# Two transformer blocks on one core: both directions of a recurrence level in one product, head norms and rotations in rounds

## The chip, the cores and the metric

The program runs on one core of a Trainium2 chip, in one launch. The metric is the time of one execution in microseconds (us) as the device measures it. TensorE (PE) multiplies, VectorE (DVE) and ScalarE (ACT) work on the elements, GpSimd (POOL) makes a part of the low halves and starts some loads, and SyncE (SP) starts the weight loads.

## The reference

The input has 256 tokens of width 1024, and a context has another 256. A first block (feed-forward, attention, feed-forward) comes first, then two layers of a second block. The change touches the second block only. Cut to what matters there:

```python
def gla_chunked(q, k, v, logf, s0):        # both directions; heads of 128, chunks
    g = cumsum(logf)
    o = (q * exp(g)) @ state + tril((q*decay) @ k.T) @ v
def hgrn_readout(o, g_raw, norm_g):
    return rms_norm(o, norm_g) * silu(g_raw)

for l in range(2):                         # second_block
    ...                                    # h = adaln_norm(x), hc = adaln_norm(context)
    q = apply_axial_rope(rms_norm(heads(q_raw), q_norm_g[l]), rope)   # heads of 64
    k = apply_axial_rope(rms_norm(heads(k_raw), k_norm_g[l]), rope)
    o_a = window_attention(q, k, v, kc, vc, sink)
    o_h, _, _ = hgrn_bidir(hgrn_q(qh_raw), kf, lff, kb, lfb, vh, s_f, s_b)
    o_hr = hgrn_readout(o_h, gh_raw, hgrn_norm_g[l])
    o_f = fourier_mix(four_raw)
    y = (sigmoid(gate_raw) * [o_f, o_a, o_hr] @ w_branch[l]).sum() @ w_out[l]
    x = x + gate2 * y
    x = x + gate5 * square(relu(adaln_norm(x) @ w_ff1[l])) @ w_ff2[l]
```

In layer 0 the context goes through the same steps as the tokens (512 columns in all); in layer 1 only its keys, values and final states are needed, so that most products there have 256 columns.

## The kernel before

**Weights.** Each fp32 weight block of 128x1024 is loaded into `wr` by SP (four buffers), ACT copies it to `wh` (high half, line 419) and DVE or POOL subtracts to get `wl` (low half, line 435; three buffers of each). A product is then three matmuls, lines 452, 455 and 457: high x high, high x low, low x high. ACT and the subtracting engine run two blocks ahead of PE. Which engine makes a low half depends on a place in the stream: `self.W.step(("pool on", l))` gives all blocks behind it to POOL.

**Order.** PE, ACT and DVE each have a program of their own, written out by hand and joined by semaphores. Every engine executes in its own order. `Ring` hands out buffers in turn: `main` and `aux` are four PSUM banks each, `tm` has three SBUF buffers, `rm` has one. Layer l does, in this order:
1. forget gates, queries and values of the recurrence;
2. the **recurrence levels** (`pe_recurrence`, `act_recurrence`, `dve_recurrence`). Level lv joins blocks of 2^lv tokens, for directions z = 0 and 1. For each z, PE multiplies K[z] by one half of the columns of Q[z] (line 1579, eight 128x64 products per sequence; layer 0 has two sequences, tokens and context). DVE scales Q[z] and K[z] by the forget factors (`dve_raise`, lines 1636 and 1639), writes the products into `AT` under a mask (`dve_pairs_out`, line 1664) and joins the factors (`dve_join`, line 1652). Level 7 (line 1572) and the states and outputs (`pe_outputs`) follow;
3. `pe_gate_h`, then the **head stage**: four readouts (norm of the recurrence's output, times a gate), values, five heads (K at j = -1, Q at 0 to 3: tile, norm, rotation), four tiles for the Fourier branch, and the Fourier products;
4. the **units** of the attention (`pe_units`: 16 with a row of scores each, in layer 0 eight more for the context), then the branches, the output and the feed-forward.

**Filling.** The 24 gate tiles of a layer depend on nothing in stages 2 to 4, and so fill holes: `Fill` deals them out in halves of 12 matmuls. `inside(n)` gives up to n halves in the recurrence until `last` (24 halves in layer 0, 32 in layer 1), `all` gives two. `OUT_FILLS` are the halves within `pe_outputs`. In the levels each z is followed by one half, in layer 1 for z = 1 by two.

**Head stage.** `pipeline(gens, 3, fill.all)` keeps three generators alive and calls each in turn, each call followed by up to two halves. A norm is: square by ACT (`act_scale`), a column sum by PE (line 1761), scale and offset by DVE out of PSUM (line 1789), Ln and Exp by ACT (lines 1778, 1780), one Newton step by DVE (lines 1792, 1794, 1796) and the product with gain and root (line 1800). A head is first copied out of PSUM (line 1880). Its rotation is one PE product (line 1863) and three DVE operations (lines 1888, 1892, 1894). `pe_head` after its norm reads:

```python
yield
...
w.wait_ge(*self.c("s_v").at((key, 4)))
ins = e.matmul(self.aux.item((key, "turn"))[:, 0:256], self.const["perm"], dst[:, 0:256], ...)
```

so that PE waits for the end of that head's DVE chain. `fill.all` has used up the gate halves by the second head of either layer.

## Time and profile before

| | us |
|---|---|
| median of 3 runs | 2222.09 |
| lowest, highest | 2217.89, 2223.20 |
| profiled execution | 2222.47 |
| its span, first to last instruction | 2220.7 |
| PE busy in the span | 2063.4 (93%) |
| DVE / ACT / POOL busy | 1275.5 / 926.2 / 597.6 |
| mean granted TensorE clock | 0.966 |

The span is 1.8 us shorter than the execution's own time, which is 0.4 us over the median. "Busy" of PE counts matmuls from start to modelled end, also when they run at the lower clock (1.2 instead of 2.4 GHz), so a stretch can be 100% busy and still slow. The page's second part shows where the clock was below 1. The rows on which the prediction rests follow behind the change.

### The profile page before, as it was taken

The page shows a single profiled execution, that of the slowest core. Times are in us where ns is not written, and L with a number is a line of the kernel's source. Part 1 is how long each engine was busy: PE and PEld are TensorE (multiplying, and loading weights), DVE is VectorE, ACT ScalarE, POOL GpSimd, SP SyncE. Part 2 cuts the span into 40 slices and gives each one's busy share as a digit, 9 for nine tenths or more (in the row PEclk, how much of TensorE's full clock was granted, in tenths as well). Part 3 has the DMA queues.
Part 4 walks back from the last instruction along what each step waited for, and adds up shares of the span by engine and source line. Part 5 has one row for each costly group of instructions (what it writes and reads, how often), then busy time and mean ns, then how long its engine had stood idle before and what let it go on. Part 6 is the DMA issues. An engine that isn't in the chain of part 4 may idle for free.

```text
span 2220.7 us, 31129 instructions
## 1 busy us (share of the span) xinstructions
PE 2063.4 (93%) x12564; PEld 1803.7 (81%) x12564; DVE 1275.5 (57%) x1973; ACT 926.2 (42%) x1497; POOL 597.6 (27%) x341
## 2 busy tenths in 40 slices
PE   7799788899989999989899899999999996888999
PEld 7799676799978998867578788888778986578999
DVE  5578896578855860343774583353367735575410
ACT  5344335455445123431553442243263342455643
POOL 0211000000000001432024355455400043046887
PEclk9899999899989999999899999999999999899999
DMA  7887371366722111211013244465422332024554
GB/s 260 248 274 259 128 243 44 119 236 218 257 86 95 48 48 67 93 69 48 1 57 114 95 152 142 152 206 192 161 90 91 114 115 85 20 92 143 185 190 153
DMA packets 84640, 299.21 MB, mean 135 GB/s; under 512 B 9993, under 2 KB 13201, under 8 KB 84113
## 3 DMA queue, kind: packets, MB, share of 16 engines
q1 hardware_dynamic: 64512, 231.76, 30.4%
q0 software_dynamic: 17280, 60.88, 8.6%
q10 hardware_dynamic: 2704, 4.57, 0.6%
q8 instruction: 100, 1.64, 0.3%
q14 instruction: 44, 0.35, 0.1%
HBM read 296.11 MB, written 4.11 MB: 135 GB/s over the span
## 4 chain that ended last, share of the span: by engine, by line
PE 81%; DVE 9%; ACT 4%; issue 2%; DMA 2%; POOL 2%; ACTq 0%; DVEq 0%; POOLq 0%
PE ps L457 21%; PE ps L452 21%; PE ps L455 21%; PE ps L1579 3%; PE ps L1056 2%; PE ps L1016 1%; PE ps L1033 1%; DVE wl L435 1%; PE ps L959 1%; PE ps L964 1%; PE ps L961 1%; PE ps L536 1%; DMA naskew<-narel 1%; POOL wl L435 1%; ACT wh L419 1%
## 5 line engine op out<-in xcount | busy, mean ns | idle before, releaser
L452 PE MATMUL ps<-HH,wh 128*128 128x256 f32 (+1 forms) x2336 | 769.9, 330 | 25.3 <-ACT HH L1284 10.7
L457 PE MATMUL ps<-HH,wl 128*128 128x256 f32 (+1 forms) x2336 | 757.2, 324 | 26.4 <-DVE wl L435 23.1
L435 POOL TENSOR_TENSOR wl<-wr,wh 128x1024 fp32r<-128x1024 f32 x214 | 519.8, 2438 | 918.1 <-ACT wh L419 903.6
L455 PE MATMUL ps<-HL,wh 128*128 128x256 f32 (+1 forms) x2336 | 756.7, 324 | 1.4 <-DVE HL L1300 1.4
L419 ACT ACTIVATE wh<-wr 128x1024 fp32r<-128x1024 f32 x440 | 460.1, 1052 | 338.1 <-PE ps L457 300.2
L452 PEld LDWEIGHTS ps<-HH,wh 128*128 128x128 f32 x2336 | 453.9, 194 | 66.0 <-issue 25.7
L457 PEld LDWEIGHTS ps<-HH,wl 128*128 128x128 f32 x2336 | 453.4, 194 | 61.6 <-DVE wl L435 25.0
L455 PEld LDWEIGHTS ps<-HL,wh 128*128 128x128 f32 x2336 | 453.6, 194 | 38.3 <-DVE HL L1300 3.4
L435 DVE TENSOR_TENSOR wl<-wr,wh 128x1024 fp32r<-128x1024 f32 x226 | 274.3, 1223 | 148.7 <-ACT wh L419 146.7
L457 PE MATMUL ps<-HIDH,wl 128*128 128x512 f32 (+1 forms) x512 | 173.1, 338 | 0.0
L452 PE MATMUL ps<-HIDH,wh 128*128 128x512 f32 (+1 forms) x512 | 172.8, 338 | 0.0
L455 PE MATMUL ps<-HIDL,wh 128*128 128x512 f32 (+1 forms) x512 | 172.3, 336 | 0.0
L2119 DVE SCALAR_TENSOR_TENSOR X<-ps,MOD,X 128x256 f32<-128x256 f32 x64 | 28.8, 480 | 246.8 <-PE ps L457 246.8
L805 POOL DMA_DIRECT2D WM<-wmod x68 | 37.7, 554 | 412.4 <-DVE MOD L832 372.9
L832 DVE CUSTOM_DVE_ANT_0 PROD<-WM,COND 128x1024 f32<-128x1024 f32 x104 | 130.3, 1261 | 1.3
L455 PEld LDWEIGHTS ps<-HIDL,wh 128*128 128x128 f32 x512 | 96.1, 188 | 11.8
L452 PEld LDWEIGHTS ps<-HIDH,wh 128*128 128x128 f32 x512 | 96.1, 188 | 11.7
L457 PEld LDWEIGHTS ps<-HIDH,wl 128*128 128x128 f32 x512 | 96.0, 188 | 11.7
L457 PE MATMUL ps<-NHH,wl 128*128 128x256 f32 x352 | 98.7, 280 | 0.2 <-DVE wl L435 0.2
L452 PE MATMUL ps<-NHH,wh 128*128 128x256 f32 x352 | 98.4, 280 | 0.0
L455 PE MATMUL ps<-NHL,wh 128*128 128x256 f32 x352 | 98.1, 279 | 0.0
L2186 DVE TENSOR_TENSOR HIDL<-tm,HIDH 128x512 fp32r<-128x512 f32 (+1 forms) x64 | 75.3, 1176 | 37.9 <-ACT HIDH L2170 37.9
(250 smaller groups left out, 2759.1 us busy)
## 6 DMA issues: line engine op xcount, KB each, us to landing
wr<-wstream SPq DMA_DIRECT2D x440, 512.0 KB, 3.3
WM<-wmod POOLq DMA_DIRECT2D x68, 512.0 KB, 3.9
X<-wmod POOLq DMA_DIRECT2D x28, 512.0 KB, 5.4
NAB<-naskew POOLq DMA_DIRECT2D x16, 128.0 KB, 7.1
dilskew<-lines POOLq DMA_DIRECT2D x1, 2048.0 KB, 22.5
DILB<-dilskew POOLq DMA_DIRECT2D x2, 1024.0 KB, 12.6
COND<-cond ACTq DMA_DIRECT2D x2, 1024.0 KB, 4.8
CT<-consts POOLq DMA_DIRECT2D x1, 1152.0 KB, 9.6
```

Source lines behind the costliest of these rows:

```text
L419: ins = e.activation(self.WH[i % NSPL][:, :], self.WR[n % NRAW][:, :], ACT.Copy)
L435: ins = e.tensor_tensor(self.WL[i % NSPL][:, :], self.WR[n % NRAW][:, :], self.WH[i % NSPL][:, :].bitcast(F32), ALU.subtract)
L452: e.matmul(out, wh, xh, start=i == 0, stop=False)
L455: e.matmul(out, wh, xl, start=False, stop=False)
L457: ins = e.matmul(out, wl, xh, start=False, stop=i == n_k - 1)
L536: ins = e.matmul(self.aux.item((key, "sum"))[:, 0:T], self.ones, self.tm.item((key, "sq", i))[:, 0:T], start=i == 0, stop=i == n - 1)
L805: e.dma_start(self.mod_buffer(z, i), src).then_inc(self.mod_sem[i], 16)
L832: ins = e.tensor_tensor_reduce(out=P, in0=self.mod_buffer(z, i), in1=S, scale=1.0, scalar=0.0, op0=ALU.mult, op1=ALU.add, accum_out=self.M ...
L1056: ins = e.matmul(b[off:off + 64, 128 * u.a:128 * u.a + 128], self.V2[:, c, off:off + 64], p[:, 128 * c:128 * c + 128], start=c == 0, stop= ...
L1579: ins = e.matmul(b[:, c:c + 64], K[:, h, at:at + 128], self.side(Q[:, h, at:at + 128], 1 << lv, 1 - z), start=True, stop=True)
L2119: ins = e.scalar_tensor_tensor(out=self.X[:, d, sl], in0=self.main.item(k)[:, sl], scalar=self.MOD[:, l, mod_i + d, c:c + 1], in1=self.X[: ...
L2186: ins = e.tensor_tensor(hl[:, f - nf * part, :], v, hh[:, f - nf * part, :].bitcast(F32), ALU.subtract)
```

## The change

**Levels 0 to 6, one product for both directions.** A new mixed K lies in `R`: for each block of the level, the K of direction 0 or 1 (`act_mixed_k`, two ACT copies per level, which wait for the level before). `Q[0]` and `Q[1]` now lie side by side as `QQ`, and `mixed_q` reads them alternately by blocks. Per sequence and half, PE does four 128x128 products (line 1567 of the new file) in place of two times four 128x64. DVE raises both K first, then both Q; the masked copies are whole (4x128 columns, `r_cp` per s and a).

**Fewer halves inside.** `last` goes from (24, 32) to (16, 24) halves; the levels get `REC_FILLS`, `OUT_FILLS` depends on the layer. `fill.some` gives two halves per round in layer 0 and one in layer 1, up to 44, and the units get what is left.

**Rounds.** `pipeline` starts one generator per round, calls each live one once per round, the new one before the last, and fills once per round. The Fourier tiles move into the readouts, the order is Q0, Q1, K, values, Q2, Q3. The norm uses a mean matrix (`mean128`, `mean64`); Ln reads PSUM with eps as bias; the four DVE operations (lines 1823 to 1830 of the new file) read PSUM where needed, and the copy (line 1880) and the scaling (line 1789) are gone. Mean, root, DVE chain and rotation of a head fall in successive rounds.

**Low halves.** `("pool on", l)` moves from before the head stage to behind the units: DVE makes those 48 low halves (POOL has 167 in place of 215, DVE 274 in place of 226).

```diff
-OUT_FILLS = (2, 2, 2)
+REC_FILLS, OUT_FILLS = ((2, 1, 2, 1, 2, 1, 2), (2, 3, 2, 3, 2, 3, 2)), ((1, 1, 1), (2, 2, 1))
...
-        for lv in range(8):
-            for z in range(2):
-                K, Q = self.K[z], self.Q[z]
-                w.wait_ge(*self.c("r_up").at((l, lv, z)))
-                for s in self.seqs(l):
...
-                        for a in range(2):
-                            at = 256 * s + 128 * a
-                            for h in range(4):
-                                c = 64 * (4 * a + h)
-                                ins = e.matmul(b[:, c:c + 64], K[:, h, at:at + 128],
-                                               self.side(Q[:, h, at:at + 128], 1 << lv, 1 - z), start=True, stop=True)
...
-                fill(1 + z * l)
+        for lv in range(7):
+            w.wait_ge(*self.c("r_km").at((l, lv)))
+            w.wait_ge(*self.c("r_up").at((l, lv, 1)))
+            for s in self.seqs(l):
+                for a in range(2):
...
+                    for h in range(4):
+                        ins = e.matmul(self.aux.item(key)[:, 128 * h:128 * h + 128], self.R[:, h, at:at + 128],
+                                       self.mixed_q(h, at, 1 << lv), start=True, stop=True)
+                    ins.then_inc(*self.c("r_mm").mark((l, lv, s, a)))
+            fill(REC_FILLS[l][lv])
...
+    def mixed_q(self, h, at, hh):
+
+        ap = self.QQ[:, 0, h, at:at + 128]
+        return bass.AP(ap.tensor, ap.offset, [list(ap.ap[0]), [2 * hh, 64 // hh], [2048 + hh, 2], [1, hh]])
...
+    def act_mixed_k(self, e, w, l, lv):
+
+        T = 256 if l else 512
+        w.wait_ge(*self.c("r_mm").at((l, lv - 1, self.seqs(l)[-1] if lv else 0, 1)))
+        for z in range(2):
+            for x in ([self.c("r_ku").at((l, lv, z))] if lv else self.forget_done(l)):
+                w.wait_ge(*x)
+            ins = e.activation(self.head_side(self.R[:, :, 0:T], 1 << lv, z), self.head_side(self.K[z][:, :, 0:T], 1 << lv, z),
+                               ACT.Copy)
+        ins.then_inc(*self.c("r_km").mark((l, lv)))
...
+        for lv in range(7):
             for z in range(2):
-                self.dve_raise(e, w, l, lv, z)
-                if lv < 7:
-                    for s in self.seqs(l):
-                        self.dve_pairs_out(e, w, l, lv, z, s)
-                    self.dve_join(e, w, l, lv, z)
-                fill(1 + z * l)
...
+                self.dve_raise_k(e, w, l, lv, z)
+            for z in range(2):
+                self.dve_raise_q(e, w, l, lv, z)
+            for s in self.seqs(l):
+                for a in range(2):
+                    self.dve_pairs_out(e, w, l, lv, s, a)
+            for z in range(2):
+                self.dve_join(e, w, l, lv, z)
+            fill(REC_FILLS[l][lv])
...
-        e.activation(r, v, ACT.Ln, scale=-2.0).then_inc(*self.c("s_a").mark((key, 0)))
+        e.activation(r, self.aux.item((key, "mean"))[:, 0:T], ACT.Ln, bias=self.vec("eps", 0)).then_inc(
+            *self.c("s_a").mark((key, 0)))
...
+    def dve_scale(self, e, w, key, T, g, v, src, dst):
...
+        e.scalar_tensor_tensor(out=v, in0=m, scalar=EPS, in1=r, op0=ALU.add, op1=ALU.mult).then_inc(*sv.mark((key, 0)))
...
+        e.scalar_tensor_tensor(out=v, in0=v, scalar=-0.5, in1=r, op0=ALU.mult, op1=ALU.mult).then_inc(*sv.mark((key, 1)))
...
+        e.scalar_tensor_tensor(out=r, in0=v, scalar=1.5, in1=r, op0=ALU.add, op1=ALU.mult).then_inc(*sv.mark((key, 2)))
...
+        e.scalar_tensor_tensor(out=dst, in0=src, scalar=g, in1=r, op0=ALU.mult, op1=ALU.mult).then_inc(*sv.mark((key, 3)))
...
-        self.W.step(("pool on", l))
         self.pe_gate_h(e, w, l, T, rT)
-        pipeline([self.pe_readout(e, w, l, h, T) for h in range(4)], 3, fill.all)
-        pipeline([self.pe_values(e, w, l, keys)] + [self.pe_head(e, w, l, j, T, keys) for j in range(-1, 4)]
-                 + [self.pe_four_in(e, w, l, g, T, rT) for g in range(4)]
-                 + [self.pe_fourier(e, w, l, g, T, self.rings["p2"]) for g in range(4)], 3, fill.all)
+        pipeline([self.pe_readout(e, w, l, h, T, rT) for h in range(4)]
+                 + [self.pe_head(e, w, l, j, T, keys) for j in (0, 1, -1)] + [self.pe_values(e, w, l, keys)]
+                 + [self.pe_head(e, w, l, j, T, keys) for j in (2, 3)]
+                 + [self.pe_fourier(e, w, l, g, T, self.rings["p2"]) for g in range(4)], fill.some)
         self.pe_units(e, w, layer_units(l), self.unit_rings(2), lambda u: self.layer_qk(l, u),
                       [self.c("hd_cp").at(("v2", l))], fill.all)
+        self.W.step(("pool on", l))
...
+    def some(self):
+
+        for _ in range(min(2 if self.last == 16 else 1, 44 - self.n)):
+            self.half()
...
-def pipeline(gens, width, fill):
+def pipeline(gens, fill):
+
 
     gens, active = list(gens), []
     while gens or active:
-        if gens and len(active) < width:
+        turns = list(active)
+        if gens:
             active.append(gens.pop(0))
-        for g in list(active):
+            turns.insert(max(len(turns) - 1, 0), active[-1])
+        for g in turns:
             if next(g, "end") == "end":
                 active.remove(g)
-            fill()
+        fill()
```

PE in the levels of layer 0 before: one direction's products of two sequences, 12 matmuls of a half gate tile, the other direction's products (Q_87 and Q_88 are the two Q, K_85 and K_86 the two K).

```order
L1579 MATMUL ps<-Q_87,K_85 128x64 x16
L452 MATMUL ps<-HH,wh 128x512
L455 MATMUL ps<-HL,wh 128x512
L457 MATMUL ps<-HH,wl 128x512
...
L1579 MATMUL ps<-Q_88,K_86 128x64 x16
```

The same place after, with the waits of the first and the later groups of four:

```order
L1567 MATMUL ps<-QQ,R 128x128 [waits s_r_cp,s_r_up,s_r_km]
L1567 MATMUL ps<-QQ,R 128x128 x3
L1567 MATMUL ps<-QQ,R 128x128 [waits s_r_cp]
...
L452 MATMUL ps<-HH,wh 128x512
L455 MATMUL ps<-HL,wh 128x512
L457 MATMUL ps<-HH,wl 128x512
```

Sixteen 128x128 products stand for 32 of 128x64. The start of a level now waits for DVE's raised Q (`r_up`), for ACT's mixed K (`r_km`) and for the masked copies (`r_cp`), once per level instead of twice.

DVE between two heads of layer 1 before: norm, product with the root, copy of the next head out of PSUM, rotation of the last.

```order
L1789 TENSOR_SCALAR tm<-ps 128x256 [waits s_s_mm]
L1792 TENSOR_TENSOR tm<-tm,rm 128x256 [waits s_s_a]
L1794 TENSOR_TENSOR tm<-tm,rm 128x256 [waits s_s_v]
L1796 SCALAR_TENSOR_TENSOR rm<-tm,rm 128x256 [waits s_s_v]
L1800 SCALAR_TENSOR_TENSOR Q_101<-Q_101,V,rm 128x256 [waits s_s_v]
L1880 COPY Q_101<-ps 128x256 [waits s_dense]
L1888 TENSOR_TENSOR tm<-ps,CT 128x256 [waits s_hd_mm,s_hd_v]
L1892 TENSOR_TENSOR Q_101<-Q_101,CT 128x256 [waits s_s_v]
L1894 TENSOR_TENSOR Q_101<-Q_101,tm 128x256 [waits s_hd_v]
```

DVE in one round of heads of layer 1 after:

```order
L1823 SCALAR_TENSOR_TENSOR Q_100<-ps,rm 128x256 [waits s_s_a]
L1826 SCALAR_TENSOR_TENSOR Q_100<-Q_100,rm 128x256 [waits s_s_v]
L1828 SCALAR_TENSOR_TENSOR rm<-Q_100,rm 128x256 [waits s_s_v]
L1830 SCALAR_TENSOR_TENSOR Q_100<-ps,V,rm 128x256 [waits s_s_v]
L435 TENSOR_TENSOR wl<-wr,wh 128x1024 [waits s_hi,s_dense] x3
L1942 TENSOR_TENSOR tm<-ps,CT 128x256 [waits s_hd_mm]
L1946 TENSOR_TENSOR Q_100<-Q_100,CT 128x256 [waits s_s_v]
L1948 TENSOR_TENSOR Q_100<-Q_100,tm 128x256 [waits s_hd_v]
```

The rotation belongs to the head one round further on; low halves stand where POOL made them before.

PE at the same two places, first before and then after (line 452 opens a tile, line 457 needs the low half):

```order
L1863 MATMUL ps<-Q_101,CT 128x256 [waits s_s_v,s_hd_cp]
L1761 MATMUL ps<-tm,CT 128x256 [waits s_s_sq]
L452 MATMUL ps<-HH,wh 128x256 [waits s_hi]
...
L457 MATMUL ps<-HH,wl 128x256 [waits s_lo_pool]
...
L1863 MATMUL ps<-Q_101,CT 128x256 [waits s_s_v,s_hd_v]
```

```order
L452 MATMUL ps<-HH,wh 128x256 [waits s_hi,s_s_v]
...
L457 MATMUL ps<-HH,wl 128x256 [waits s_lo_dve]
...
L1915 MATMUL ps<-Q_100,CT 128x256
L452 MATMUL ps<-HH,wh 128x512 [waits s_gate]
...
L1796 MATMUL ps<-tm,CT 128x512 [waits s_s_sq]
```

The rotation product (line 1863, now 1915) no longer has a wait of its own here: the tile ahead of it already waited for that DVE chain (`s_s_v`), because it takes the PSUM bank that the chain gives back.

## Rows read from the trace of the kernel before

**Rows 1.** Page, part 4: the chain that ended last, by engine.

```profile
PE 81%; DVE 9%; ACT 4%; issue 2%; DMA 2%; POOL 2%; ACTq 0%; DVEq 0%; POOLq 0%
```

**Rows 2.** Windows by stage: length, busy us of each engine, PEclk, DMA, GB/s.

```profile
730.95:819.40 88.45, 88.45 (x617) 81.64 (x616) 67.36 (x75) 10.80 (x14) 0.00 (x0) 1.00 0.12 42
856.00:1054.10 198.10, 186.66 (x785) 147.82 (x783) 68.31 (x88) 60.79 (x85) 63.36 (x26) 0.98 0.21 72
1054.10:1130.10 76.00, 68.75 (x353) 43.92 (x352) 58.53 (x155) 46.19 (x136) 0.00 (x0) 0.89 0.00 1
1700.39:1755.50 55.11, 55.11 (x479) 55.11 (x478) 53.76 (x68) 13.62 (x21) 0.00 (x0) 1.00 0.27 96
1755.50:1905.60 150.10, 125.31 (x825) 114.56 (x823) 63.27 (x93) 54.71 (x91) 53.06 (x22) 0.94 0.29 99
1905.60:1957.50 51.90, 45.50 (x225) 27.48 (x224) 36.84 (x103) 31.36 (x88) 0.00 (x0) 0.87 0.00 1
```

**Rows 3.** Timeline, PE, levels: start, us, line, tile, count.

```profile
724.64 3.74 PE L1555 MATMUL ps<-Q,R 128*128 128x128 f32 x32
...
730.95 3.69 PE L1579 MATMUL ps<-Q,K 128*128 128x64 f32 x32
734.44 0.48 PE L452 MATMUL ps<-HH,wh 128*128 128x512 f32 x1
...
737.26 3.69 PE L1579 MATMUL ps<-Q,K 128*128 128x64 f32 x32
...
1702.10 0.36 PE L452 MATMUL ps<-HH,wh 128*128 128x256 f32 x1
...
1703.61 1.89 PE L1579 MATMUL ps<-Q,K 128*128 128x64 f32 x16
```

**Rows 4.** Timeline, DVE, levels of layer 0.

```profile
735.82 1.22 DVE L1636 TENSOR_TENSOR K<-K,F 128x1024 f32<-128x1024 f32 x1
736.95 2.47 DVE L1664 COPY_PREDICATED AT<-LM,ps 128x512 f32<-128x512 uint8 x2
...
746.69 1.20 DVE L435 TENSOR_TENSOR wl<-wr,wh 128x1024 fp32r<-128x1024 f32 x1
...
762.49 1.31 DVE L1664 COPY_PREDICATED AT<-LM,ps 128x512 f32<-128x512 uint8 x2
```

**Rows 5.** Waits of PE, head stages: total, times, longest; layer 0, then 1.

```profile
PE ps L1863 <- DVE Q L1800: 6.6, 4, 1.8
...
PE ps L1863 <- DVE Q L1800: 9.9, 4, 3.0
PE ps L1863 <- DVE K L1800: 4.4, 1, 4.4
PE ps L1761 <- ACT tm L1771: 3.8, 3, 1.6
...
PE ps L457 <- POOL wl L435: 2.4, 3, 1.0
```

**Rows 6.** Timeline, all engines, one head of layer 1.

```profile
1860.04 0.42 DVE L1888 TENSOR_TENSOR tm<-ps,CT 128x256 f32<-128x256 f32 x1 [0.59 <-PE ps L1863]
...
1863.50 0.43 DVE L1796 SCALAR_TENSOR_TENSOR rm<-tm,rm 128x256 f32<-128x256 f32 x1
1863.64 2.48 POOL L435 TENSOR_TENSOR wl<-wr,wh 128x1024 fp32r<-128x1024 f32 x1 [4.81 <-PE ps L457]
1863.96 2.44 DVE L1800 SCALAR_TENSOR_TENSOR Q<-Q,V,rm 128x256 f32<-128x256 f32 x1
...
1867.85 0.42 DVE L1888 TENSOR_TENSOR tm<-ps,CT 128x256 f32<-128x256 f32 x1 [1.11 <-PE ps L1863]
```

**Rows 7.** Timeline, PE, first units of layer 1.

```profile
1913.06 1.09 PE L1033 MATMUL ps<-CT,s 128*128 128x128 f32 x4 [5.46 <-DVE s L1150]
1914.08 2.07 PE L1016 MATMUL ps<-K,Q 64*128 64x512 f32 x2
...
1929.51 1.12 PE L1016 MATMUL ps<-K,Q 64*128 64x512 f32 x2
```

More of the change, by code:

```diff
@@ new lines, in dve_raise @@
+    def dve_raise(self, e, M, z, hh, u, c0, c1):
+        if c1 - c0 == 512:
+            m, f = (t.rearrange("p h t -> p (h t)") for t in (M[:, :, :], self.F[z][:, :, :]))
+            m, f = self.side(m, hh, u), self.side(f, hh, 1 - u)[:, :, 0]
+            return e.tensor_tensor(m, m, bc(f, 2, hh), ALU.mult)
+        m = self.head_side(M[:, :, c0:c1], hh, u)
+        f = self.head_side(self.F[z][:, :, c0:c1], hh, 1 - u)[:, :, :, 0]
+        return e.tensor_tensor(m, m, bc(f, 3, hh), ALU.mult)
@@ L1750, in act_out, with pe_scale @@
             self.aux.release(key, self.c("r_ca"), (l, "out", s, hp))
-    def pe_scale(self, e, w, key, T, over):
+    def pe_scale(self, e, w, key, T, mean):
         self.tm.take((key, "sq"))
         yield
-        self.aux.take((key, "sum"))
-        for x in self.aux.before((key, "sum")):
+        self.aux.take((key, "mean"))
+        for x in self.aux.before((key, "mean")):
             w.wait_ge(*x)
         w.wait_ge(*self.c("s_sq").at(key))
-        ins = e.matmul(self.aux.item((key, "sum"))[:, 0:T], self.const[over], self.tm.item((key, "sq"))[:, 0:T],
+        ins = e.matmul(self.aux.item((key, "mean"))[:, 0:T], self.const[mean], self.tm.item((key, "sq"))[:, 0:T],
                        start=True, stop=True)
@@ L1765, in pe_scale @@
         self.rm.take(key)
-        self.tm.take((key, "v"))
+        yield
     def act_scale(self, e, w, key, T, src, ready):
@@ L1805, in pe_gate_h @@
+        self.rm.release(key, sv, (key, 3))
     def pe_gate_h(self, e, w, l, T, rhs):
@@ L1820, in act_gate_h, with pe_readout @@
             self.main.release(key, self.c("gh"), (l, h))
-    def pe_readout(self, e, w, l, h, T):
-        yield from self.pe_scale(e, w, ("ro", l, h), T, "ones")
+    def pe_readout(self, e, w, l, h, T, rhs):
+        c = W_IN["four"] + 128 * h
+        self.pe_tile(e, w, l, ("four", l, h), [(c, c + 128)], T, rhs)
+        yield from self.pe_scale(e, w, ("ro", l, h), T, "mean128")
+        self.tm.take(("ro", l, h))
+        yield
+        yield
     def act_readout(self, e, w, l, h, T):
+        self.make_high(e, w, (("four", l, h), 0))
         yield from self.act_scale(e, w, ("ro", l, h), T, self.O[:, h, 0:T], self.o_done(l))
+        yield
         w.wait_ge(*self.c("o_gate").at((l, h)))
@@ L1829, in act_readout @@
         ins.then_inc(*self.c("oh_hi").mark((l, h)))
+        yield
     def dve_readout(self, e, w, l, h, T):
         o, key = self.O[:, h, 0:T], ("ro", l, h)
-        yield from self.dve_scale(e, w, key, T, 128, self.vec("hgrn_norm_g_2", l), o)
-        w.wait_ge(*self.c("s_v").at((key, 4)))
+        self.make_low(e, w, "lo_dve", (("four", l, h), 0))
+        for x in self.o_done(l):
+            w.wait_ge(*x)
+        w.wait_ge(*self.c("dense").at(("four", l, h)))
+        e.tensor_copy(self.FR[:, h, 0:T], self.main.item(("four", l, h))[:, 0:T]).then_inc(*self.c("four").mark((l, h)))
+        self.main.release(("four", l, h), self.c("four"), (l, h))
+        yield
+        yield
+        for x in self.tm.before(key):
+            w.wait_ge(*x)
+        self.dve_scale(e, w, key, T, self.vec("hgrn_norm_g_2", l), self.tm.item(key)[:, 0:T], o, o)
+        self.tm.release(key, self.c("s_v"), (key, 2))
+        w.wait_ge(*self.c("s_v").at((key, 3)))
         w.wait_ge(*self.c("gh").at((l, h)))
         e.tensor_tensor(o, o, self.GH[:, h, 0:T], ALU.mult).then_inc(*self.c("o_gate").mark((l, h)))
+        yield
         w.wait_ge(*self.c("oh_hi").at((l, h)))
```

218 lines of the change are left out of this document (102 added, 116 removed).

## Prediction

> **What bounds the kernel now.** I read the page's chain by engine first [rows 1]: PE carries 81% of it, so what counts is PE's work, PE's idle time, and PE's clock. Then I took one window for each stage the change touches [rows 2]: window length, busy time of each engine, granted clock. They split the case in two.
>
> - Levels: 88.45 us in layer 0, 55.11 in layer 1, PE busy for all of both at clock 1.00. Here only fewer matmuls, or fewer gate halves, can shorten PE; DVE with 67.36 and 53.76 us busy is right behind, in layer 1 only 1.35 us behind.
> - Head stages and units: PE is idle for 198.10 - 186.66 = 11.4 us (heads, layer 0), 76.00 - 68.75 = 7.3 (units), 150.10 - 125.31 = 24.8 (heads, layer 1) and 51.90 - 45.50 = 6.4 (units), 49.9 us in all. The clock was below 1: busy time times (1 - clock) is time lost to it, 3.7, 7.6, 7.5 and 5.9 us, 24.7 in all. Together 74.6 us are the most that better order there can give, unless a matmul disappears.
>
> The waits [rows 5] say what the heads wait for: the rotation product on the last operation of the same head's norm (6.6 us in layer 0; 9.9 + 4.4 in layer 1), the mean on ACT's square (3.8), low halves of POOL (2.4). One head in the timeline [rows 6] shows how such a wait gets long: a whole period is 1867.85 - 1860.04 = 7.8 us, and line 1800, an operation of 0.43 us like its neighbour, takes 2.44 us after it started 0.32 us behind a low half of POOL. At the units [rows 7] PE starts after a gap of 5.46 us and then runs the same two matmuls in 2.07 us that later take 1.12: the clock's lower level after the gap.
>
> **Levels, PE's side.** The products of one direction take 734.44 - 730.95 = 3.49 us in layer 0 for 32 matmuls of 128x64, and 728.13 - 724.64 = 3.49 was the pace of 32 of 128x128 just before [rows 3] (the rows show 3.7 us with the drain). So a product costs the same with twice the columns, about 0.109 us, and halving the number halves the time: seven levels go from 48.9 to 24.4 us. In layer 1 one direction takes 1.7 us (half as many), 23.9 goes to 12.0. A half gate tile takes 737.26 - 734.44 = 2.82 us and 1703.61 - 1702.10 = 1.51 [rows 3]. 3 of 14 leave the levels of layer 0, 4 of 21 those of layer 1; they are moved, not saved: 8.5 and 6.0 us come back later.
>
> **Levels, DVE's side.** PE would need 24.4 + 11 x 2.82 = 55.4 us in layer 0 and 12.0 + 17 x 1.51 = 37.7 in layer 1. DVE needs more, so it is now the bound. Its raises stay (28 per layer; 1.13 us from one start to the next) and its joins; low halves, one per two gate halves at 1.14 us [rows 4], fall by 1.5 and 2. The masked copies stay in number, but the first two levels' took 1.12 us each (2.47 for two) and later ones 0.62 (1.31 for two) [rows 4]; they now write whole tiles, like later ones, if the strided writing was the reason: -0.5 x 8 = -4.2 us, in layer 1 -2.1. From both sides: they save nothing, or these figures. DVE: 67.4 - 1.7 - 4.2 = 61.5 us, and 53.8 - 2.3 - 2.1 = 49.4 us. Levels of layer 0 with two halves are PE's again (3.5 + 5.6 = 9.1 us against 8.8 for DVE), +1.2. So 62.7 and 49.4 us against 88.45 and 55.11. With the moved halves the gain is 25.7 - 8.5 = **17.3 us** in layer 0 and 5.7 - 6.0 = **0** in layer 1. PE then idles 7 and 12 us in them.
>
> ACT's new copies (two per level, of 128x1024 or half) find an engine that is busy 10.80 of 88.45 and 13.62 of 55.11 us [rows 2]. I cost them at nothing: they run while DVE raises Q, which is waited for anyway, and behind them on ACT stand only high halves that are made ahead. Exposed, they would cost the level's start: a second per level, 14 us, as the far bound.
>
> PE's idling has a price where it drops the clock. Level stages show 1.00 without gaps; units show 0.87 and 0.89 with gaps of 5 us. The new gaps are 1 us per level in layer 0 and 1.7 in layer 1, and I allow **-3 us** for them, between nothing and the whole layer-1 stage at half rate (below).
>
> **Head stages.** A round in layer 1 is one tile (24 products of 0.12 us, 2.9 us), one gate half (1.5), a mean and a rotation: about 4.7 to 5.2 us of PE. DVE has four norm operations and three rotation operations of 0.43 us, with 0.46 between starts (3.2), and 1.5 low halves (1.7): 4.8 to 5.4 us. Before, a head took 7.8 us [rows 6], since its steps followed each other within one call and the halves had run out by the second head. Now each wait has a whole round in between: what PE waits for in [rows 5] is over before PE asks. The four operations per norm replace five and a copy, which DVE no longer does. The 48 low halves come to DVE, 26 in layer 0 and 22 in layer 1: +30 and +25 us on an engine that is busy 68.31 of 198.10 and 63.27 of 150.10 us [rows 2]: it stays under PE's time as a whole. With POOL silent no DVE operation is stretched as in [rows 6]; I found such stretches of about 10 and 16 us in the two stages, and that pays more than half of the added work. I keep a remainder of idle and clock loss: 4 us in layer 0, where a round has two halves of 2.82 and DVE has slack, 10 in layer 1, where the two engines are level. Gains: 11.4 + 3.7 - 4 = **11.1** and 24.8 + 7.5 - 10 = **22.3 us**. Bounds of the remainder: 0, and all of it.
>
> The Trainium skill, "SBUF — State Buffer", section "SBUF: two separate sides", says that a GpSimd operation and a DVE operation with two SBUF inputs exclude each other for a whole instruction. The trace agrees [rows 6], 2.44 us beside a POOL operation of 2.48. By that rule moving the low halves removes every stretch.
>
> **Units.** They get 4 halves in layer 0 and 9 in layer 1 where they had none. PE has something to do while the first scores go through ACT and DVE: the gap of 5.46 us [rows 7] is filled by three or four halves (1.5 us each), and if the clock stays up, so does the next stretch. Gains 7.3 + 7.6 - 3 = **11.9** and 6.4 + 5.9 - 2 = **10.3 us**.
>
> **Sum.** 17.3 + 0 - 3 + 11.1 + 22.3 + 11.9 + 10.3 = 69.9 us. Against the profiled execution of 2222.5 us, which is 0.4 us above the median, that gives **2152 us**. With the remainders between nothing and twice what I took (19 us), and the level terms between their bounds of 6 us, this case alone spans 2140 to 2172.
>
> **Rivals.**
> - *The rounds of heads are longer than PE's work.* If DVE's round is some 1.3 us longer than I count (copies of the values and Fourier tiles fall in the same rounds, and a low half can stand in front of a chain), the 15 rounds of layer 1 cost 20 us: 2172. For it: DVE and PE are level at about 5 us. Against it: DVE's busy share of 42% today, stretches included.
> - *The clock falls in the levels of layer 1.* PE idles about 1.7 of 7 us there. At half rate its work per level is 3.4 + 7.3 = 10.7 us in place of 7: +24 us, 2176. For it: clock 0.87 in the units of layer 1 with gaps [rows 2, 7]. Against it: the heads of layer 1 idle for 17% of their time and still have 0.94.
> - *PE reads alternating blocks at half pace.* Q is now read in pieces of 1, 2, 4 columns from two arrays. Before, it was read with a stride too, but from one. At 0.218 us per product the levels of layer 0 grow by about 18 us and of layer 1 by 3: 2173.
> - *The levels stay as long as before.* That the halved products bring no time since something in the new order (all copies, then joins, then raises) holds the level at 12.6 and 7.9 us: the 17.3 are lost, 2170.
> - *The stretched DVE operations stay.* If POOL is not their cause, DVE has 26 us of them beside the added low halves: about 2179.
> - *Slower: the rounds close into a chain.* The tile ahead of the rotation product waits for the DVE chain that frees its PSUM bank, and the rotation product stands behind it on PE. If that chain belongs to the same round, a round is PE's work plus the chain: four operations and Ln, Exp of ACT, about 3.4 us in layer 1 (8.6 us in place of 5.2) and 3.6 in layer 0 (15.4 for 11.8). Over 15 and 14 rounds that is +51 and +50: 2253. It decides the sign from 2.4 us per round. Against it: that DVE chain was issued a round earlier by the order of the code, and half a round of PE work lies between.
>
> [...]
>
> **How the numbers follow.** The sum as it stands 0.60 (own range 2140 to 2172); longer rounds 0.15; the clock 0.07; PE's reading 0.07; levels unchanged 0.03; stretches 0.03; slower 0.03. The rest, 0.02, is for less than 0.3% either way. All but the last two are over 0.3% faster, which is about what a measurement of this kernel can tell from no change: 0.95 faster, 0.02 same, 0.03 slower. The range must reach to the middle rivals and hold the sum's lower end: 2138 to 2178.
>
> **What the new profile would show.** Level products (line 1567) of about 0.109 us each; a level of layer 0 every 9 us and of layer 1 every 7; DVE busy nearly throughout, PE idle 7 and 12 us. In the head stages: POOL at nothing, no DVE operation of 256 columns over 0.5 us, PE idle of some us only, waits on `s_a` and `s_v` gone, rounds of 5.2 and 11.8 us. In the units: no gap of 5 us at the start, clock near 1. Wrong would be: a level's length above DVE's work in it (a wait between the engines), PE waiting for line 435 of DVE in layer 1, or a clock under 0.95 in the levels.

## The result, and the profile after

| | before | after |
|---|---|---|
| median, us | 2220.24 (4 runs) | 2170.69 (4 runs) |
| lowest, highest | 2217.89, 2223.20 | 2166.70, 2171.76 |
| profiled execution | 2222.47 | 2171.41 |
| PE busy in the span | 2063.4 | 2025.4 |
| POOL / DVE busy | 597.6 / 1275.5 | 490.6 / 1277.9 |

The ratio is 0.9776, with a 95% interval of 0.9760 to 0.9792: 49.6 us faster. The forecast was 2152 us, 70 us faster, and the range 2138 to 2178. The direction and the range held, and 20 us of the expected gain are missing.

The same windows as in [rows 2], of the kernel after: window, its length, busy us of PE, of weight loads, DVE, ACT and POOL, then the granted clock, DMA share and GB/s. Layer 0, in order: levels, level 7 and outputs, head stage with its tiles, units.

```profile
735.11:798.81 63.70, 57.99 (x356) 51.66 (x357) 61.58 (x76) 21.41 (x23) 0.00 (x0) 1.00 0.12 42
798.81:826.13 27.32, 27.32 (x165) 24.57 (x164) 6.16 (x7) 10.53 (x17) 0.00 (x0) 1.00 0.18 59
826.13:1036.53 210.40, 195.55 (x815) 157.00 (x813) 78.78 (x101) 62.87 (x88) 0.00 (x0) 0.96 0.20 70
1036.53:1118.83 82.30, 79.33 (x401) 51.79 (x400) 61.03 (x157) 49.38 (x140) 0.00 (x0) 0.94 0.04 14
```

Layer 1, the same four stages:

```profile
1688.80:1736.61 47.81, 41.99 (x317) 41.10 (x317) 46.89 (x60) 18.84 (x30) 0.00 (x0) 0.93 0.26 89
1736.61:1758.61 22.00, 21.46 (x157) 20.28 (x157) 9.11 (x13) 8.76 (x14) 0.00 (x0) 1.00 0.28 96
1758.61:1848.28 89.67, 86.93 (x611) 81.57 (x609) 55.26 (x90) 43.08 (x72) 0.00 (x0) 1.00 0.37 124
1848.28:1906.48 58.20, 56.14 (x334) 38.19 (x333) 42.65 (x108) 36.54 (x97) 0.00 (x0) 1.00 0.13 46
```

Side by side, with before cut at the same instructions (us, and in brackets PE's idle time and the time lost to the clock, busy time times 1 - clock):

| stage | before | after |
|---|---|---|
| layer 0: levels | 88.5 (0, 0) | 63.7 (5.7, 0) |
| layer 0: outputs | 35.5 | 27.3 |
| layer 0: heads | 199.2 (11.4, 3.8) | 210.4 (14.9, 7.8) |
| layer 0: units | 76.0 (7.3, 7.6) | 82.3 (3.0, 4.8) |
| layer 1: levels | 55.0 (0, 0) | 47.8 (5.8, 2.9) |
| layer 1: outputs | 23.9 | 22.0 |
| layer 1: heads | 126.3 (24.8, 7.1) | 89.7 (2.7, 0) |
| layer 1: units | 51.9 (6.4, 5.9) | 58.2 (2.1, 0) |
| sum | 656.3 | 601.4 |

So 54.9 us come from these stages, and the profiled execution is 51.1 shorter; the other 3.8 us lie in parts that the change doesn't touch, and no run here shows their cause (the first level starts at 730.95 before, at 735.11 after; in the profiles of the experiments below it starts anywhere from 733.74 to 742.45, once at 729.76). The levels paid in both layers, and layer 1 gave nearly all that its head stage and units had to give. Layer 0's heads and units gave nothing. Six gate halves more fall in these two windows, 16.9 us of work, and they grew by 17.5 (from 275.2 to 292.7); the idle and slow time is the same 30 us as before.

Where PE waits in layer 0's head stage, after (us in total, times, longest):

```profile
PE ps L452 <- DVE Q L1830: 9.7, 3, 4.8
PE ps L452 <- DVE K L1830: 4.2, 1, 4.2
```

These four waits are new; in the same view of the kernel before no tile (line 452) waits for DVE. The chain of waits around the first shows what ends it (start, us, engine, tile and line):

```profile
920.56 0.24 PE ps L457
920.82 0.60 ACT GB L1510
921.42 0.53 ACT OHH L1865
921.97 0.69 DVE OHL L1889
922.66 0.61 DVE Q L1823
923.30 0.70 DVE Q L1826
924.02 0.70 DVE rm L1828
924.75 0.76 DVE Q L1830
925.56 0.79 PE ps L452
```

PE ends the gate tile of the round before at 920.80. ACT copies it (line 1510), and only then comes to the high half of a readout (1865), which stands behind that copy in its order. DVE's low half (1889) waits for this, and the norm of Q0 (1823 to 1830), whose inputs had been ready since Exp ended at 916.75, stands behind it. PE's next head tile waits for line 1830: the norm now reads the tile in PSUM, so this operation is what frees the bank. PE stands still for 4.77 us, and its next matmuls start every 0.43 us, not 0.23, until 931.8. The other two long waits are alike, with the rotation (1942 to 1948) in place of the low half: PE's rotation product, then DVE's rotation, then the norm behind it, then PE's tile. DVE is busy for only 78.8 of the stage's 210.4 us; it is the order of its work, and not the amount, that makes PE wait (the first experiment tests it).

Why two rounds only lie between: `main` has four banks. A round of layer 0 takes two of them, the head's tile and a whole gate tile, so that the tile of round r + 2 gets the bank of the head of round r, and it stands at the head of the very round in which DVE does that head's norm. In layer 1, with one half per round, a round takes one and a half.

### The profile page after: what moved, and what is told of

Read it like the earlier page. It is cut to its first block, busy times and chain, and to the rows that moved or that the text cites. A ratio compares the mean times of both kernels' runs of the same rounds, so it can differ in the third digit from the quotient of the medians.

```text
span 2169.6 us, 30444 instructions
## 1 busy us (share of the span) xinstructions
PE 2025.4 (93%) x12228; PEld 1769.0 (82%) x12228; DVE 1277.9 (59%) x1993; ACT 949.1 (44%) x1525; POOL 490.6 (23%) x293
## 4 chain that ended last, share of the span: by engine, by line
PE 77%; DVE 12%; ACT 4%; issue 3%; DMA 2%; POOL 2%; ACTq 0%; DVEq 0%; POOLq 0%
PE ps L457 21%; PE ps L452 21%; PE ps L455 21%; DVE wl L435 2%; ACT wh L419 1%; PE ps L1016 1%; PE ps L536 1%; DVE K L1656 1%; PE ps L1056 1%; PE ps L1033 1%; PE ps L959 1%; PE ps L961 1%; PE ps L964 1%; DMA naskew<-narel 1%; POOL wl L435 1%
## 5 line engine op out<-in xcount | busy, mean ns | idle before, releaser
L435 POOL TENSOR_TENSOR wl<-wr,wh 128x1024 fp32r<-128x1024 f32 x166 | 413.0, 2497 | 969.6 <-ACT wh L419 964.9
L457 PEld LDWEIGHTS ps<-HH,wl 128*128 128x128 f32 x2336 | 452.9, 194 | 61.5 <-DVE wl L435 26.9
L435 DVE TENSOR_TENSOR wl<-wr,wh 128x1024 fp32r<-128x1024 f32 x274 | 333.2, 1224 | 235.8 <-ACT wh L419 234.1
```

Source lines behind the costliest of these rows:

```text
L435: ins = e.tensor_tensor(self.WL[i % NSPL][:, :], self.WR[n % NRAW][:, :], self.WH[i % NSPL][:, :].bitcast(F32), ALU.subtract)
L457: ins = e.matmul(out, wl, xh, start=False, stop=i == n_k - 1)
```

## Experiments

Each kernel is the changed kernel with one edit, unless said otherwise. Times are medians, with the ratio to before and its 95% interval; the changed kernel's own is 2170.7 us (0.9760 to 0.9792).

### Is it the order inside DVE's round?

```diff
+        if rev and len(turns) > 3:
+            turns.insert(0, turns.pop(len(turns) - 3))
         for g in turns:
```

`rev` is true for DVE's rounds alone, in both layers.

> The changed kernel with one difference: in a round of the head stage DVE does the norm's four operations (lines 1823 to 1830) ahead of the rotation of the head before and of the readout's low half, in place of behind them. Theory (a chain closes through the PSUM bank): a head's tile keeps its bank of `main` until line 1830, a round of layer 0 takes two of the four banks (a head's tile and a whole gate tile), so that the bank is asked for again two rounds later, at the head of the very round in which DVE frees it, behind operations that wait for that round's work of PE and ACT. With the norm first, it runs while PE does the last round's gate halves: PE's waits of 4.8, 4.2 and 4.2 us for line 1830 in layer 0 fall below 1 us each, and the clock loss behind them goes. Time 2171 - 13 - 3 = about 2155 us. Rival (DVE has too much work in a round, 26 low halves among it): the order inside a round changes nothing, the waits stay in sum, 2171 us. Rival (the heads wait longer elsewhere, since the rotation is now late): 2165 to 2175.

Measured: 2149.9 us, 0.9690 (0.9668 to 0.9711). Waits of PE, and the windows of heads and units, in layer 0:

```profile
PE ps L452 <- DVE Q L1830: 1.8, 2, 1.1
PE ps L2009 <- DVE p L2031: 0.9, 1, 0.9
PE ps L452 <- DVE K L1830: 0.6, 1, 0.6
```

```profile
824.76:1016.42 191.66, 188.26 (x815) 151.94 (x813) 78.51 (x101) 62.90 (x88) 0.00 (x0) 1.00 0.23 77
1016.42:1097.85 81.43, 78.18 (x401) 51.30 (x400) 60.92 (x157) 49.59 (x140) 0.00 (x0) 0.96 0.04 14
```

The waits fall from 13.9 to 2.4 us and the clock is 1.00, so that the head stage takes 191.7 us in place of 210.4. DVE has exactly the same work. The rival of too much work is out. The sum of the four stages falls from 383.7 to 364.1 us in layer 0; in layer 1 the same edit brings 2.6 us.

### Is it the bank?

Two kernels leave DVE's order as it is and change when the bank is asked for, or when it is given back.

```diff
-        for _ in range(min(2 if self.last == 16 else 1, 44 - self.n)):
+        for _ in range(min(1, 44 - self.n)):
```

> The changed kernel with one gate half per round of layer 0's head stage in place of two; the 14 or so halves left over come in the units, two beside each unit. Theory (a bank asked for again two rounds later): now a round takes 1.5 banks of the four, as in layer 1, so that a bank comes back after 2.67 rounds and DVE has had its round for the norm. The waits of 13 us in sum for line 1830 in layer 0 fall below 4 us though DVE's order is unchanged. The units have more than enough halves. About 2155 us, if rounds of half the length do not open other waits. Rival (DVE has too little time per round): a shorter round has less room for the same chain, so the waits stay or grow, 2171 to 2190 us.

Measured: 2146.1 us, 0.9656 (0.9629 to 0.9684). Heads and units of layer 0:

```profile
826.58:981.57 154.99, 154.83 (x671) 125.17 (x669) 71.45 (x95) 53.63 (x76) 0.00 (x0) 1.00 0.22 75
981.57:1093.82 112.25, 108.36 (x545) 75.68 (x544) 68.35 (x163) 58.67 (x152) 0.00 (x0) 1.00 0.12 38
```

PE waits for 0.16 us in the whole head stage, though each round has less work beside the same chain. Heads and units together take 267.2 us in place of 292.7.

```diff
         self.make_low(e, w, "lo_dve", (key, 0))
+        if l == 0:
...
+            w.wait_ge(*self.c("dense").at(key))
+            e.tensor_copy(dst, self.main.item(key)[:, 0:TT]).then_inc(*self.c("hd_cp").mark((l, j)))
+            self.main.release(key, self.c("hd_cp"), (l, j))
...
```

With it ACT's square reads the copy, and the norm reads the copy and takes a buffer of `tm` for its steps.

> The changed kernel with one part undone in layer 0 alone: a head's tile is copied out of PSUM by DVE as soon as it is ready (as by line 1880 before), which gives the bank back, and square and norm read the copy in SBUF. DVE's order inside a round is that of the changed kernel. Theory (the bank is what PE waits for): the waits of PE's head tiles for line 1830 in layer 0 are gone, for five more DVE operations of 0.7 us that lie beside PE's work: -13 us of waits, -3 or so of clock loss, 2155 us. Rival (PE waits for the round's DVE chain in another way, or DVE lacks the time): waits of the same sum come up at another line, 2168 to 2175 us.

Measured: 2148.9 us, 0.9675 (0.9645 to 0.9706). Waits of PE in heads and units of layer 0:

```profile
PE ps L1033 <- DVE s L1150: 2.8, 4, 1.2
PE ps L2026 <- DVE p L2048: 0.9, 1, 0.9
```

No wait for line 1830 is left. Five operations more on DVE, and 21.8 us less. Leaving out the copy cost this time only together with two banks per round and DVE's order: each of the three edits alone takes nearly all of the waits away.

The third kernel makes the same thing happen in layer 1, with two halves per round there:

```diff
-        for _ in range(min(2 if self.last == 16 else 1, 44 - self.n)):
+        for _ in range(min(2, 44 - self.n)):
```

> The changed kernel with two gate halves per round in layer 1 too, so that a round takes two banks there as in layer 0. Theory (bank reuse after two rounds): layer 1 gets the waits that layer 0 has, a norm's and a rotation's operations of 256 columns each: 4 x 0.46 + 1.2 = about 3 us, three or four times, 8 to 12 us, and clock loss behind them; besides, halves run out early and the units start with none (a gap as before, 5 us, with its clock loss). Time 2171 + 10 to + 20 = about 2185 us. Rival (the layer-0 waits come from 512 columns and two Fourier halves, not from the banks): the head stage of layer 1 keeps its 3 us of waits; only the units lose something, 2171 to 2177 us.

Measured: 2185.7 us, 0.9838 (0.9811 to 0.9866). Waits of PE in heads and units of layer 1:

```profile
PE ps L452 <- DVE Q L1830: 6.1, 2, 3.1
PE ps L452 <- DVE K L1830: 4.4, 1, 4.4
PE ps L1033 <- DVE s L1150: 3.0, 4, 1.3
```

Three waits of up to 4.4 us for line 1830 at tiles, 10.5 us in sum, where the changed kernel has one of 0.9; clock 0.94 in the heads. So the chain doesn't need layer 0's 512 columns. The stages of layer 1 take 234.5 us in place of 217.7. The feared gap at the units is only 3.0 us, since 4 halves are still left for them; that part of the expectation was wrong.

### What did POOL's low halves cost?

The changed kernel with the low halves of head stages and units back on POOL (`self.W.step(("pool on", l))` ahead of `pe_gate_h` again):

> The changed kernel, but POOL makes the 48 low halves of head stages and units again, as before. Theory (POOL stretches DVE's operations): DVE operations of 0.43 to 0.75 us that start beside a low half of POOL take about 2 us more, as at 1863.96 before. DVE's busy time in the layer-1 head stage: less 25 us of low halves, plus 15 or so of stretches; the rounds have slack only partly, so 5 to 15 us slower, about 2181 us. Rival (the stretches have another cause): no such operations in this kernel either, DVE is lighter, 2171 us or less. Rival (low halves on DVE are what makes layer 0's waits): those waits of 13 us go, about 2158 us.

Measured: 2188.7 us, 0.9857 (0.9840 to 0.9874). DVE operations of layer 1's head stage up to 1848 us (busy us, mean ns), first of this kernel, then of the changed one:

```profile
L1826 DVE SCALAR_TENSOR_TENSOR tm<-tm,rm 128x256 f32<-128x256 f32 x4 | 5.2, 1300 | 0.1
L1830 DVE SCALAR_TENSOR_TENSOR O<-O,V,rm 128x256 f32<-128x256 f32 x4 | 4.0, 999 | 0.1
```

```profile
L435 DVE TENSOR_TENSOR wl<-wr,wh 128x1024 fp32r<-128x1024 f32 x21 | 25.6, 1223 | 29.2 <-ACT wh L419 29.2
...
L1830 DVE SCALAR_TENSOR_TENSOR O<-O,V,rm 128x256 f32<-128x256 f32 x4 | 1.9, 485 | 0.1
...
L1826 DVE SCALAR_TENSOR_TENSOR tm<-tm,rm 128x256 f32<-128x256 f32 x4 | 1.7, 424 | 0.1
```

```profile
1762.35:1864.58 102.23, 91.33 (x610) 84.78 (x608) 46.38 (x69) 43.01 (x72) 50.86 (x21) 0.95 0.33 109
```

The same operation takes 1300 ns on average with POOL at work beside it and 424 without. The head stage of layer 1 takes 102.2 us in place of 89.7, and that of layer 0 214.7 in place of 210.4, where the same four waits grow to 18.9 us. Worth 18 us in all, more than expected.

Which operations are stretched can be seen in this kernel too (start, us; POOL's line is two low halves in a row):

```profile
1805.71 4.91 POOL L435 TENSOR_TENSOR wl<-wr,wh 128x1024 fp32r<-128x1024 f32 x2 [2.86 <-ACT wh L419]
1808.28 0.41 DVE L1823 SCALAR_TENSOR_TENSOR tm<-ps,rm 128x256 f32<-128x256 f32 x1
1808.72 2.18 DVE L1826 SCALAR_TENSOR_TENSOR tm<-tm,rm 128x256 f32<-128x256 f32 x1
```

Both DVE operations start while POOL is at work. Line 1826, with both operands in SBUF, takes five times its usual time and ends 0.3 us after POOL. Line 1823, which reads one operand in PSUM, takes its usual 0.41 us. Line 1830 of K, which reads its tile in PSUM, keeps its time too: 0.75 us from 1835.21 on, while POOL makes a low half from 1834.76 to 1837.38.

The kernel before with this part alone:

> The kernel before with one part of the change alone: the 48 low halves of the head stages and units are DVE's instead of POOL's. Theory (POOL's stretches made the long waits for line 1800): no DVE operation of 2.4 us is left in the head stage, PE's waits for line 1800 fall from 9.9 and 4.4 to 6 us in layer 1 and from 6.6 to 4 in layer 0, less clock loss behind them: 8 to 14 us faster, about 2210 us. Rival (DVE's own low halves now stand in front of the chain): the waits stay or grow, 2220 to 2228 us. Rival (the stretches have another cause): they remain beside the added work, over 2225 us.

Measured: 2205.3 us, 0.9935 (0.9916 to 0.9953), 14 us faster than before. Waits of PE in layer 1's head stage and units:

```profile
PE ps L1761 <- ACT tm L1771: 10.0, 8, 1.6
PE ps L1033 <- DVE s L1150: 5.5, 1, 5.5
PE ps L1974 <- DVE p L1996: 3.3, 4, 0.9
PE ps L1863 <- DVE K L1800: 2.4, 1, 2.4
PE ps L1908 <- DVE tm L1923: 1.5, 1, 1.5
PE ps L1863 <- DVE Q L1800: 1.2, 2, 0.6
```

The waits for the norm (line 1863) fall from 14.3 us [rows 5] to 3.6; those for the square (line 1761), behind the same chain, grow from 3.8 to 10.0. In layer 1 the head stage takes 115.7 us in place of 126.3. The gap at the units stays, as it should.

### What sets the levels?

```diff
-                    for h in range(4):
+                    for h in (0, 1, 2, 3, 0, 1, 2, 3):
```

> The changed kernel with each product of levels 0 to 6 done twice into the same place, so that PE has as many of them as before. Theory (DVE bounds the levels, PE's halved work is hidden where it is below DVE's): layer 0's levels need PE for 48.9 + 31.0 = 79.9 us in place of 55.4, against 63.7 measured: +16; layer 1's 23.9 + 25.7 = 49.6 against 48.2 measured: +2 to +5 with hand-overs. Sum +18 to +21, about 2190 us. Rival (each level is a chain of products, then DVE, then products, with nothing beside): every added microsecond counts, +24.4 + 12 = +36, 2207 us. Rival (PE is nowhere near the bound in the levels): 2171 us.

Measured: 2195.8 us, 0.9892 (0.9873 to 0.9910), +25 us. Levels of layer 0 and of layer 1:

```profile
734.31:820.66 86.35, 85.01 (x580) 78.73 (x581) 62.44 (x76) 20.93 (x23) 0.00 (x0) 1.00 0.10 31
```

```profile
1709.32:1761.24 51.92, 51.92 (x428) 51.65 (x429) 49.09 (x65) 18.60 (x29) 0.00 (x0) 1.00 0.26 82
```

+22.7 and +4.1 us. In layer 1 it is the +2 to +5 expected: the added work is hidden until PE is busy for the whole stage. In layer 0 my account of PE was 5 us too small: with 79.9 us expected, PE is busy for 85.0. Most of that is level 0, where 64 products at 0.165 us are 10.6 us, and not 7.0. Its 32 products, and those of the other levels (count: least, median and longest ns, first and last start):

```profile
L1567 PE MATMUL ps<-QQ,R x32: 333/337/422, 735.1 to 740.4; 128*128 128x128 f32 x32
```

```profile
L1567 PE MATMUL ps<-QQ,R x192: 270/275/348, 746.0 to 793.2; 128*128 128x128 f32 x192
```

337 ns in place of 275, with pieces of one column read in turn from the two directions. The next kernel reads pieces of two at level 0:

```diff
-                                       self.mixed_q(h, at, 1 << lv), start=True, stop=True)
+                                       self.mixed_q(h, at, max(2, 1 << lv)), start=True, stop=True)
```

> The changed kernel, but level 0 reads Q in pieces of two columns, alternately from the two directions, in place of pieces of one, so that its output isn't the reference's. All waits and all work stay. Theory (the read of single columns from two arrays is slow): the 32 products of level 0 in layer 0 fall from 5.3 us to the 3.8 of level 1, in layer 1 from 2.6 to 1.9: 337 ns of one to 275 or 280 ns. The time falls by 1 to 2 us at most, within what can be measured, since DVE sets the level. Rival (level 0 is slowed by K or by waits): its products keep 337 ns.

Measured: 2173.4 us, 0.9791 (0.9771 to 0.9810), no difference to the changed kernel. The products of level 0:

```profile
L1567 PE MATMUL ps<-QQ,R x32: 282/283/387, 735.4 to 739.2; 128*128 128x128 f32 x32
```

283 ns, as at level 1, which reads pieces of two in both kernels: the pattern of the read is what slows them. Against the pace of the later levels, single columns cost 1.8 us of PE's time in layer 0 and 0.9 in layer 1. Most of that lies beside DVE's work: the levels of layer 0 take 62.9 us in place of 63.7, those of layer 1 47.9 and 47.8.

### What did the halves for the units bring?

> The changed kernel, but in layer 0 the head stage takes all gate halves (up to 48) and none are left for the units. Theory (the halves fill the hole before the first scores are ready): the gap of about 6 us ahead of the first line 1033 is back, and with it the lower clock for some units, so that the units take 76 us where they need 71 without it; the head stage takes 11.3 us more for the same halves. Sum +5 us, about 2176 us. Rival (the units start well without halves, since line 1016 of the next units can run ahead): 2171 us.

Measured: 2174.5 us, 0.9796 (0.9779 to 0.9813), 3.8 us over the changed kernel; the two intervals overlap. The trace is clearer:

```profile
PE ps L1033 <- DVE s L1150: 7.1, 3, 6.3
```

The wait for the first scores is back at 6.3 us and the units take 76.06 us at clock 0.89, just as before, where without their 11.3 us of halves they would have taken 71.0. So the four halves save 5 us there. Over both stages less is left of it: the heads take 218.5 us in place of 210.4, 8.1 more where 11.3 were expected, and heads and units together 294.5 in place of 292.7. More of them, taken from the last rounds of the heads, did not help (on top of the kernel with the norm first):

> The kernel with the norm ahead of the rotation on DVE, and 8 gate halves in place of 4 kept for the units of layer 0 (the head stage stops at 40). Theory (the units start with too few halves there: gaps of 1.2 and 1.1 us and clock 0.81 and 0.85 in the next 20 us): the gaps are filled and the clock stays at 1.00 as in layer 1, -3 - 3 us; the last Fourier rounds lose their halves, where waits for line 2031 of 0.9 us each come up, +2 to +4. Time 2150 - 2 to 4 = about 2147 us. Rival (the last rounds of the head stage need the halves as much as the units do): 2150 us or more.

Measured: 2154.4 us, 0.9700 (0.9669 to 0.9731), no gain on 2149.9. In its trace the four stages of layer 0 take 367.4 us in place of 364.1: the last rounds of the head stage wait for line 2031 for 2.7 us (0.9 before), and the units stay at clock 0.96. The rival was right.

### A version that beats both

One half per round in layer 0, and the norm first:

> The changed kernel with both: one gate half per round in layer 0, and DVE's norm ahead of the rotation in both layers. Each removed layer 0's waits by itself, so they don't add up there (358 us for the four stages of layer 0 with the first, 364 with the second). In layer 1 the order alone took 2.6 us off the head stage (89.67 to 87.03). Theory: 2146 - 3 = about 2143 us. Rival (with one half per round DVE's reordered rotation comes late for PE's next round): 2146 us or more.

Measured: 2144.9 us, 0.9661 (0.9646 to 0.9675). Layer 1's head stage takes 87.0 us in place of 89.7, as with the order alone; against one half per round alone (2146.1) the times can't tell it apart.

To that, two halves in every level of layer 0 and none in its outputs (`REC_FILLS` (2, 2, 2, 2, 2, 2, 2), `OUT_FILLS` (0, 0, 0)):

> The kernel with one half per round and the norm first, and in layer 0 two gate halves in each of the seven levels (14 in place of 11) and none in the output stage behind them. Theory (DVE bounds the levels and PE has 5.7 us of idle time in them): the levels grow by 1.5 low halves and by the three levels that PE now sets at 9.1 us, 63.7 to 66 or 67; the output stage loses 8.5 us of work and gets waits of its own in place of them, 27.3 to 19 to 23. Together 0 to 5 us faster than 2143. Rival (the halves hid the copies between the output products): the output stage stays at 25 or more and the sum is 0 to 2 us slower than 2143.

Measured: 2137.6 us, 0.9632 (0.9618 to 0.9647), the fastest, though its interval just touches that of 2144.9; in the traces the four stages of layer 0 take 351.7 us in place of 357.8. Levels, outputs and heads of layer 0:

```profile
739.09:804.82 65.73, 65.73 (x393) 58.54 (x394) 63.60 (x76) 24.28 (x27) 0.00 (x0) 1.00 0.17 57
804.82:826.71 21.89, 21.89 (x142) 19.98 (x140) 4.00 (x8) 7.93 (x14) 0.00 (x0) 1.00 0.08 25
826.71:978.55 151.84, 151.84 (x659) 122.99 (x657) 71.25 (x95) 53.02 (x75) 0.00 (x0) 1.00 0.23 77
```

PE is busy for all of the levels, which take 65.7 us with 14 halves (63.7 with 11). The outputs' window has one half left (21.9 us) where it had three (27.3), and the third moved half came off the window of the heads (151.8 in place of 154.6). So 8.5 us of work went where it costs 2.0, and nothing new is waited for.

## Why the prediction was right in its direction, and 20 us too far

- **Levels.** PE's products at half the number, DVE as the new bound: right. Forecast 62.7 and 49.4 us, measured 63.7 and 47.8. DVE's work was forecast at 61.5 us and is 61.6; the first masked copies take 0.65 us each (2.60 for four), as assumed. The allowance of 3 us for the clock was not needed, though the clock over layer 1's levels is 0.93, under the 0.95 that the prediction named as a sign of being wrong. Nearly all of that is one level at 0.66 (second row), after a wait of 2.96 us for ACT's mixed K (line 1614), and DVE was busy for all 9.0 us of that level, so that PE's slowness is covered. ACT's copies, taken at nothing, do make PE wait in layer 1, four times and 5.6 us in all, but DVE is busy for 46.9 of the 47.8 us, so that this too costs next to nothing. PE is busy for 42.0 us there and not 37.7, and idle for 5.8 and not 12. Three levels of layer 1:

```profile
1702.60:1710.48 7.88, 4.89 (x40) 4.75 (x41) 7.88 (x10) 2.78 (x5) 0.00 (x0) 0.96 0.19 69
1710.48:1719.48 9.00, 9.00 (x52) 9.00 (x53) 9.00 (x14) 4.03 (x7) 0.00 (x0) 0.66 0.18 58
1719.48:1724.96 5.48, 4.82 (x42) 4.64 (x41) 5.48 (x7) 1.99 (x5) 0.00 (x0) 1.00 0.52 177
```

- **Layer 1, heads and units.** Right, and better than forecast: 2.7 us of idle time and none of clock loss remain in the heads where I kept 10. DVE's operations all take their short time, and rounds of about 5 us hold both engines' work. The gap at the units is gone, with the clock at 1.00.
- **Layer 0, heads: the step that failed.** I took a remainder of 4 us, "where a round has two halves of 2.82 and DVE has slack". It is 14.9 + 7.8 = 22.7 us, 18.7 more, nearly all of the 20 us that are missing. The rival of the closed chain was the right mechanism, with its two elements (a tile that waits for the chain that frees its bank, a round's work in front of it), and I set it aside with "that DVE chain was issued a round earlier by the order of the code". It was not: it is issued in the same round, behind operations that wait for that round's work. I also looked at whether DVE had time, and not at how many bank takes lie between a tile and the tile that gets its bank. The rival's own price was off too: I had it in all rounds of both layers at 3.5 us each (100 us), and it struck only where a head's tile held the bank: four times in layer 0, three at 4.2 to 4.8 us and one at 0.8, and once in layer 1, at 0.9.
- **Layer 0, units.** 7.7 us remain where I took 3: PE is idle for 3.0 us and the clock, at 0.94, takes 4.8. Too few halves would be the obvious reason, but the runs don't bear it out. With eight halves, on top of the norm first, the idle time is 3.9 us and the clock 0.96; with sixteen (one half per round in the heads) the clock is 1.00 and the idle time still 3.9. Halves all along the units keep the clock up, and what sets the idle time stays open.
- **POOL.** Right. The Trainium skill, "SBUF — State Buffer", section "SBUF: two separate sides", has an operation of DVE with two SBUF inputs and one of POOL that reads SBUF exclude each other for a whole instruction. The trace agrees: with POOL silent no stretched operation is left, with POOL back they return (1300 ns in place of 424), and those that read an operand in PSUM keep their 0.41 us.
- **Rivals.** Slower reading of alternating blocks exists at level 0 alone to any extent, 337 ns to 275 (0.165 us from start to start and not 0.218). The clock in the levels of layer 1 fell in one level of seven; by its own terms that rival's price was 26 us and not 24. The levels did not stay as they were.
- **The range.** The remainders at nothing and at twice their size, and the masked copies saving nothing, give 2134 to 2178 by the prediction's own terms; its span of 2140 to 2172 for the sum is narrower and not derived. The measured 2170.7 lies in either.

In sum, against the forecast gain of 69.9 us: heads of layer 0 -18.7, units of layer 0 -4.7, heads of layer 1 +7, levels and clock allowance +3.5, and -4 in parts that the change leaves alone: 53, for 51.1 in the profiled execution. That the miss stayed at 20 us is in part luck: the 7 us that layer 1's heads gave beyond the forecast made up for a part of layer 0.

## What to carry to other kernels

An operation that reads its input in PSUM instead of copying it out saves the copy and keeps the bank until that operation is done. Before taking the copy away, count the bank takes between a tile and the next user of its bank, find the round in which that is, and see what stands ahead of the freeing operation on its engine; if it is work of the same round, the pipeline closes into a chain however idle the engine looks. Within a round, put first what frees something that the next round's first instruction waits for.

## What the runs showed of the hardware

- A matmul of 128x128 whose moving operand is read in single columns in turn from two arrays takes 337 ns in these records where it takes 275 with pieces of four columns or more, and 283 with pieces of two (one start every 0.165 us in place of 0.109). The kernel before read every second column of one array at level 0 at the usual pace [rows 3].
- A DVE operation of 0.42 us with both inputs in SBUF takes 1.3 us on average when POOL makes low halves in the stage, and 2.2 to 2.5 when it starts early in one; with one input in PSUM it takes 0.41 us beside POOL as well. Moving 48 low halves to DVE, 59 us more work for it, made the old kernel 14 us and the new one 18 us faster.
- PE's idle gaps of 4.2 to 4.8 us are each followed by matmuls at half the pace, for 3.6 to 6.2 us; of the shorter gaps in the levels of layer 1 (0.4 to 3.0 us) only the longest was followed by such a stretch, there with the clock at 0.66 over its level. A gap's length alone does not decide. The same gap of 2.58 us in the levels of layer 0 left 32 products at 3.81 us in the changed kernel, and 5.44 in the one with pieces of two (clock 1.00 and 0.69 behind it):

```profile
772.48 3.81 PE L1567 MATMUL ps<-QQ,R 128*128 128x128 f32 x32 [2.58 <-DVE AT L1695]
771.46 5.44 PE L1567 MATMUL ps<-QQ,R 128*128 128x128 f32 x32 [2.58 <-DVE AT L1695]
```

- In the first units of layer 0, with the norm first, two gaps of 1.2 and 1.1 us lie in the first 6 us of a stretch of 20 us (1030 to 1050) whose halves have the clock at 0.81 and 0.85.
